# A two-layer decoder trunk on one core: bias put into the mixing's banks, first blocks in turns, token scales by transposes, four early units behind a normed phase

## What is computed

```python
def chunked_gmlp(h, w_in, v_g, w_s, b_s, w_out):
    uv = gelu(h @ w_in); u, v = split(uv, 2)           # 2048 x 4096
    v = rms_norm(v by group of 128 columns, v_g)
    mixed = einsum('gts,bnsgd->bntgd', w_s * causal, v) + b_s.T   # per chunk of 128 tokens
    return (u * mixed) @ w_out                          # 2048 x 2048

for layer in range(2):
    hn = rms_norm(h, pre_mix_g[layer])
    mix = chunked_gmlp(hn, ...) if layer == 0 else attention(hn, K, V) @ b_w_o
    h = h + rms_norm(mix, post_mix_g[layer])
    f = conv_ffn(rms_norm(h, pre_ffn_g[layer]), ...)
    h = h + rms_norm(f, post_ffn_g[layer])
```

## Time and profile before

| | us |
|---|---|
| median of 3 runs (2145.09 to 2146.48) | 2145.13 |
| the profiled execution | 2144.64 |
| its span | 2142.9 |
| TensorE busy | 2132.9 (100%) |
| TensorE weight loads busy | 1829.1 (85%) |
| VectorE busy | 1438.2 (67%) |
| ScalarE busy | 1012.9 (47%) |
| GpSimd busy | 72.0 (3%) |

### The profile page before, as it was taken

How to read it: one execution, slowest core, us unless ns; L and a number is a source line. 1 busy time by engine, 2 the same in 40 slices (tenths; PEclk the granted TensorE clock), 3 DMA queues, 4 the chain that set the end, 5 groups by cost and what they waited for, 6 DMA issues and landing times.

```text
span 2142.9 us, 32178 instructions
## 1 busy us (share of the span) xinstructions
PE 2132.9 (100%) x11289; PEld 1829.1 (85%) x11289; DVE 1438.2 (67%) x1766; ACT 1012.9 (47%) x1167; POOL 72.0 (3%) x97
## 2 busy tenths in 40 slices
PE   9999999999999999999999999999999999999998
PEld 7888888888888888888888888888888888888887
DVE  5676577787877774444765675577877778774444
ACT  5444454444444444443644574464444444444442
POOL 0510010000000000000000000010000000000000
PEclk9999999999999999999999999999999999999999
DMA  8865566666666666555566544656666666666664
GB/s 254 232 188 176 184 179 192 192 188 181 194 192 186 186 207 203 191 191 181 188 190 190 175 153 155 206 170 195 186 177 200 191 189 189 180 220 192 195 195 149
DMA packets 210414, 406.27 MB, mean 190 GB/s; under 512 B 13440, under 2 KB 15904, under 8 KB 209696
## 3 DMA queue, kind: packets, MB, share of 16 engines
q1 hardware_dynamic: 207904, 398.51, 60.9%
q0 software_dynamic: 2384, 6.70, 1.0%
q10 hardware_dynamic: 48, 0.02, 0.0%
HBM read 403.06 MB, written 2.10 MB: 189 GB/s over the span
## 4 chain that ended last, share of the span: by engine, by line
PE 98%; issue 0%; DMA 0%; DVE 0%; ACT 0%; SPq 0%; DVEq 0%; POOLq 0%; POOL 0%; ACTq 0%
PE ps L1433 37%; PE ps L1436 18%; PE ps L1447 13%; PE ps L1449 13%; PE ps L1448 13%; PE ps L1400 1%; PE ps L1403 1%; PE ps L1364 1%; PE ps L1534 1%; PE ps L1367 0%; PE ps L1608 0%; PE ps L1675 0%; PE ps L1646 0%; DMA raw<-in_a_w_in 0%; PE ps L1657 0%
## 5 line engine op out<-in xcount | busy, mean ns | idle before, releaser
L869 DVE TENSOR_TENSOR w_lo<-raw,w_hi 128x1024 fp32r<-128x1024 f32 x744 | 907.6, 1226 | 638.4 <-ACT w_hi L535 632.9
L535 ACT CAST w_hi<-raw 128x1024 fp32r<-128x1024 f32 x750 | 782.2, 1050 | 944.3 <-PE ps L1436 527.6
L1433 PE MATMUL ps<-x_parts,w_hi 128*128 128x512 f32 x3136 | 1089.3, 394 | 0.0
L1436 PE MATMUL ps<-x_parts,w_lo 128*128 128x256 f32 x3136 | 869.7, 277 | 0.0
L1433 PEld LDWEIGHTS ps<-x_parts,w_hi 128*128 128x128 f32 x3136 | 588.1, 188 | 137.1
L1436 PEld LDWEIGHTS ps<-x_parts,w_lo 128*128 128x128 f32 x3136 | 589.1, 188 | 0.0
L1447 PE MATMUL ps<-w_hi,g_parts 128*128 128x512 f32 x704 | 274.0, 389 | 0.0
L1449 PE MATMUL ps<-w_hi,g_parts 128*128 128x512 f32 x704 | 273.9, 389 | 0.0
L1448 PE MATMUL ps<-w_lo,g_parts 128*128 128x512 f32 x704 | 273.9, 389 | 0.0
L1449 PEld LDWEIGHTS ps<-w_hi,g_parts 128*128 128x128 f32 x704 | 132.1, 188 | 27.7
L1448 PEld LDWEIGHTS ps<-w_lo,g_parts 128*128 128x128 f32 x704 | 132.1, 188 | 27.5
(11 more groups left out here) (168 smaller groups left out, 1753.6 us busy)
## 6 DMA issues: line engine op xcount, KB each, us to landing
raw<-in_ffn_w_up SPq DMA_DIRECT2D x352, 512.0 KB, 3.7
raw<-in_ffn_w_down SPq DMA_DIRECT2D x176, 512.0 KB, 4.7
raw<-in_a_w_in SPq DMA_DIRECT2D x62, 512.0 KB, 4.6
raw<-in_a_w_out SPq DMA_DIRECT2D x32, 512.0 KB, 4.7
raw<-in_b_w_q SPq DMA_DIRECT2D x32, 512.0 KB, 4.6
raw<-in_w_k SPq DMA_DIRECT2D x32, 512.0 KB, 4.5
raw<-in_w_v SPq DMA_DIRECT2D x32, 512.0 KB, 4.6
raw<-in_b_w_o SPq DMA_DIRECT2D x32, 512.0 KB, 4.6
```

What stands on the lines that cost most here:

```text
L535: act.copy(w_hi[:, slot, :, :], raw[:, slot, :, :]).then_inc(unit_hi, 1)
L869: dve.tensor_tensor(w_lo[:, slot, :, :], raw[:, slot, :, :], w_hi[:, slot, :, :].bitcast(F32), ALU.subtract).then_inc(unit_split, 1)
L1433: pe.matmul(ps[:, bank + m, :], w_hi[:, slot, kk, m * P:(m + 1) * P], src[:, kt, :, :].rearrange("p a t -> p (a t)"), start=first, stop=False,
L1436: mm = pe.matmul(ps[:, bank + m, 0:T], w_lo[:, slot, kk, m * P:(m + 1) * P], src[:, kt, HI, :], start=False, stop=last, skip_group_check=True)
```

## The change

Four edits, which share names but no place in time but for the token scales.

1. **Bias.** `bias_parts` and its split go. POOL loads the bias, the same for all partitions, into `bias_wide` in four pieces during `gate_u`. ScalarE copies it into the mixing's banks (`place_bias`): four during the last block of `gate_u`, four behind it. TensorE's mixing products add to what lies there. VectorE's addition for the last u block moves in front of the first gates. The next phase waits for two gated groups instead of four.
2. **First blocks in turns.** `load_first_blocks` and `first_blocks` take units of block 0 and block 1 of `gate_v` alternately, so each x tile serves two units; three units, not two, are split half by half; VectorE makes the first cast; the stream's pieces are loaded at greater distances and turned behind units 2, 4, 8 and 12.
3. **Token scales.** `spread` transposes the scales, broadcast along the free dimension; `pre_diagonals` goes. The first one is done before the last unit of the two first blocks.
4. **Behind a normed phase.** `EARLY` = 4 and a twelfth slot; slot 2 is turned before the last tile of the normed phase. VectorE casts the third unit (`third_high`), POOL subtracts unit 1 alone, once `h` is updated in its first quarter, and VectorE unit 2. ScalarE waits for the drained bank before slot 3.

```diff
@@ POOL
+            for q in range(NB):
+                pool.wait_ge(unit_used, gate_u.unit(1) + UK * q)
+                pool.dma_start(bias_wide[:, q * TB:(q + 1) * TB, :],
+                               a_b_spatial[0:1, q * TB:(q + 1) * TB, :].to_broadcast([P, TB, P])
+                               ).then_inc(bias_loaded, 16)
...
-                    if s + 1 < len(NORMED):
-                        unit_low(BEHIND[s], half + 1)
                 if s + 1 < len(NORMED):
+                    pool.wait_ge(h_new[1], NB * s + 1)
+                    unit_low(BEHIND[s], 1)
                     pre_rsqrt(s + 1)
@@ ScalarE
+            def place_bias(g2):
+                if g2 == 0:
+                    act.wait_ge(bias_loaded, 16 * NB)
+                act.copy(ps[:, mixing_bank(g2), :].rearrange("p (g a t) -> p g a t", g=2, a=NH),
+                         bias_wide[:, 2 * g2:2 * g2 + 2, :].unsqueeze(2).to_broadcast([P, 2, NH, P])
+                         ).then_inc(bias_placed, 1)
...
+            act.wait_ge(evacuated, gate_u.block_end)
+            for g2 in range(2):
+                place_bias(G // 4 + g2)
             for g2 in range(2):
                 group_high(g2)
+                place_bias(G // 4 + 2 + g2)
+            gelu_u(LAST)
             units(a_out.first, RING - 1, RING)
-            gelu_u(LAST)
@@ ScalarE, turn_and_split
+                act.wait_ge(evacuated, ph.block0)
+                slot_high(t, (3,))
+                act.wait_ge(unit_hi, ph.first + 3)
                 units(ph.first, 3, RING)
+                slot_high(t, (4, 5))
+                slot_keep(t, (3, 4))
+                slot_high(t, (6, 7))
...
                 units(nxt.first, 0, 2)
-                slot_high(s + 1, (0, 1))
-                slot_keep(s + 1, (0,))
+                slot_high(s + 1, (0, 1, 2))
                 square(s, LAST, (1,))
+                slot_keep(s + 1, (0, 1, 2))
@@ VectorE
+            def third_high(ph):
+                dve.wait_ge(raw_loaded[2], 16 * (ph.first // RING + 1))
+                dve.wait_ge(unit_used, ph.first + 2 - RING + 1)
+                dve.wait_ge(unit_hi, ph.first + 2)
+                dve.tensor_copy(w_hi[:, 2, :, :], raw[:, 2, :, :]).then_inc(unit_hi, 1)
...
             def turn_and_split(t, ph):
-                slot_low(t, (2,))
+                gain_block(t - 1, LAST, (1,))
                 update_first(t - 1)
-                gain_block(t - 1, LAST, (1,))
-                slot_low(t, (3,))
+                slot_low(t, (3, 4))
                 update_stream(t - 1, 1, 1)
-                slot_low(t, (4,))
+                slot_low(t, (5,))
                 update_stream(t - 1, 2, 0)
                 update_stream(t - 1, 2, 1)
-                slot_low(t, (5, 6))
-                dve.wait_ge(unit_split, ph.first + EARLY)
-                units(ph.first, 3, RING)
+                slot_low(t, (6, 7))
+                dve.wait_ge(unit_split, ph.first + 2)
+                units(ph.first, 2, RING)
                 update_stream(t - 1, 3, 0)
                 update_stream(t - 1, 3, 1)
-                slot_low(t, (7,))
+                slot_low(t, (8, 9))
                 units(ph.first, RING, RING + 1)
...
             units(a_out.first, 0, RING - 1)
+            add_low(u_block(LAST), LAST + 1, column_bank(LAST % 2, 1))
             gate_group(0)
             gate_group(1)
-            add_low(u_block(LAST), LAST + 1, column_bank(LAST % 2, 1))
+            scale_tokens(u_block(LAST), gate_u.block0 + LAST, LAST + 1)
             group_low(0)
-            scale_tokens(u_block(LAST), gate_u.block0 + LAST, LAST + 1)
             group_low(1)
@@ TensorE
+                    if u == 1:
+                        turn_slots(t, (3,))
                     if u == EARLY - 1:
-                        turn_slots(t, (3, 4))
+                        turn_slots(t, (4, 5))
...
             def spread(t):
-                pe.wait_ge(diag_ready, t + 1)
+                pe.wait_ge(pre_scaled, t + 1)
                 for half in range(NH):
-                    mm = pe.matmul(ps[:, row_bank(t), half * P:(half + 1) * P], ones_r[:, :].bitcast(F32), diag[:, half, :],
-                                   start=True, stop=True)
+                    mm = pe.transpose(ps[:, row_bank(t), half * P:(half + 1) * P],
+                                      pre_scale[:, half:half + 1].to_broadcast([P, P]), ident[:, :])
...
+            TURNED_BEHIND = {2: range(4, 6), 4: range(6, 10), 8: range(10, 14), 12: range(14, KT)}
+            def first_blocks():
+                for n in range(2 * U):
+                    hb, u = n % 2, n // 2
+                    if n == 2 * U - 1:
+                        spread(0)
+                    if n < OPENING:
+                        opening_unit(n)
+                    else:
+                        pe.wait_ge(unit_split, n + 1)
+                        pe.wait_ge(x_ready, UK * u + UK)
+                        tokens_out_half(gate_v, hb, u, 0, x_parts, n % RING)
+                        tokens_out_half(gate_v, hb, u, 1, x_parts, n % RING).then_inc(unit_used, 1)
+                    turn(0, TURNED_BEHIND.get(n, ()))
...
             for g2 in range(G // 2):
-                bias = bias_parts[:, 2 * g2:2 * g2 + 2, :].unsqueeze(2).to_broadcast([P, 2, NH, P])
-                pe.matmul(ps[:, bank, :].rearrange("p (g a t) -> p g a t", g=2, a=NH), ones_r[:, :], bias,
-                          start=True, stop=False, skip_group_check=True)
+                pe.wait_ge(bias_placed, g2 + 1)
...
-            pe.wait_ge(group_gated, 4)
+            pe.wait_ge(group_gated, 2)
```

More of the change, by code:

```diff
@@ L210, in build_trunk @@
         x_loaded = [sem(f"x_loaded{c}") for c in range(KT // UK)]
-        first_loaded = [sem(f"first_loaded{u}") for u in range(2)]
+        first_loaded = [sem(f"first_loaded{n}") for n in range(3)]
+        first_cast = sem("first_cast")
         first_hi = sem("first_hi")
@@ L395, in load_pair @@
                         k = hb * ph.units + u
[L396 to L401, removed]
+                        sp.wait_ge(unit_split, i * (2 * ph.units) + (ph.first + k - RING + 1))
                         rows = ph.w[u * UK * P:(u + 1) * UK * P, bass.ds(ph.column(i, hb), BLK)]
[L403 to L407, removed]
                         sp.dma_start(raw[:, k % RING, :, :],
@@ L672, in gelu_u @@
                 act.activation(tiles, tiles, ACT.Gelu_apprx_tanh).then_inc(u_ready, 1)
-            U = gate_v.units
-            for b in range(1, NB):
-                units(gate_v.unit(b), NB - 1 if b == 1 else 0, RING)
+            def place_bias(g2):
[4 more added lines that the diff above has]
+                         ).then_inc(bias_placed, 1)
+            U = gate_v.units
+            for b in range(2, NB):
+                units(gate_v.unit(b), 0, 2)
+                if b == 2:
+                    gelu_v(0)
+                units(gate_v.unit(b), 2, RING)
                 gelu_v(b - 1)
@@ L687, in _ @@
                     gelu_u(b - 1)
+                    if b == LAST:
+                        act.wait_ge(evacuated, gate_u.block0 + LAST)
+                        for g2 in range(G // 4):
+                            place_bias(g2)
                     units(gate_u.unit(b), RING + 2, U)
-                if b == 2:
-                    act.wait_ge(bias_loaded, 16)
-                    act.wait_ge(bias_cleared, 1)
-                    act.copy(bias_parts[0:1, :, :], bias_row[:, :, :]).then_inc(bias_hi, 1)
             def group_high(g2):
@@ L1438, in columns_out, with tokens_out_half @@
                         mm.then_inc(unit_used, 1)
-            def tokens_out_half(ph, hb, u, half, src):
-                slot = (hb * ph.units + u) % RING
+            def tokens_out_half(ph, hb, u, half, src, slot=None, tiles=range(UK)):
+                slot = (hb * ph.units + u) % RING if slot is None else slot
                 t0 = half * P
-                for kk in range(UK):
+                for kk in tiles:
                     kt = UK * u + kk
@@ L1463, in last_units @@
                 for u in range(ph.units - RING, ph.units):
-                    tokens_out_half(ph, hb, u, 1, src).then_inc(unit_used, 1)
+                    tokens_out_half(ph, hb, u, 1, src, tiles=range(UK - 1))
+                    if t is not None and u == ph.units - 1:
+                        turn_slots(t, (2,))
+                    tokens_out_half(ph, hb, u, 1, src, tiles=range(UK - 1, UK)).then_inc(unit_used, 1)
                     if t is not None and u == ph.units - 2:
@@ L1560, in products @@
                     for half in range(NH):
-                        mm = pe.matmul(ps[:, half, :], x_parts[:, kt, x_part, half * P:(half + 1) * P],
-                                       w_part[:, u, kk, :], start=(kt == 0 and x_part == HI and w_part is w_hi),
-                                       stop=False)
+                        mm = pe.matmul(ps[:, token_bank(gate_v, hb, half), :],
```

(2 more changed lines are left out.)

189 lines of the change are left out of this document (76 added, 113 removed).

## The result

The changed kernel takes 2163.23 us (median of 6 runs, 2155.18 to 2164.07), the kernel before 2145.24 beside it (6 runs, 2145.09 to 2146.48): a ratio over all runs of 1.0078, 95% interval 1.0068 to 1.0088 (the medians alone give 1.0084). It is slower by 0.8%, where 2141.5 was forecast, with a range of 2138.8 to 2143.8. The profiled execution took 2164.07 around a span of 2162.3.

What follows compares the result with a forecast made beforehand. TensorE was taken as the bound, with 98% of the chain. Mixing -2.3, token scales -0.9, opening -1.4 and behind the normed phases +1.0 made -3.6, from the median 2145.13 to 2141.5 us; range 2138.8 to 2143.8.

Steps and rivals of the forecast that it cites:

- the one that I forecast and priced at 0.4: Behind each normed phase: TensorE waits 0.4 us for the low part of unit 4.
- Mixing: In the mixing, bias copied into the banks removes TensorE's bias products: 6.6 us instead of 9.0, less a 0.1 wait, gain 2.3.
- the round: In the mixing: one of eight equal parts, its eight mixing pieces taking 0.81 us without the bias product.
- The forecast wait of 0.1: In the mixing: ScalarE's fourth late bias copy ends at 194.6, TensorE wants it at 194.5, so it waits 0.1 us.
- late copies: Rival, mixing: at 0.9 us per bias copy the fourth comes at 196.0, 1.5 of 2.3 lost: 2143.0; chance 0.10.
- Token scales: At four spreadings of the scales: two transposes replace four fp32 pieces, 0.22 us less each, 0.9 in all.
- The 0.09 for a spreading: Token scales: by the skill's factor of four the 0.35 us of four pieces becomes 0.09, saving 1.0 over four spreadings.
- Opening: In the first two blocks: earlier first product 0.3, fewer waits 0.9, fewer turnings 0.2; gain 1.4 us, bounds 0.2 to 2.0.
- The burst of spatial loads: After the opening: POOL's `v_gain` and first spatial load leave at about 47, some 10 us later; cost zero, bound 1.5.
- Behind the normed phases: At three places, the new unit order costs 0.25 us each, 0.25 more behind K and V; together +1.0.
- Both forecast waits: Behind each normed phase: TensorE waits 0.2 us at unit 2's second half and 0.4 at unit 4.
- The slower rival: Behind each normed phase VectorE becomes the bound; 2149.9 us if its chain is 2.8 longer per phase; chance 0.05.

Runs made afterwards that it cites:

- only_behind: The kernel before with only the new order behind a normed phase (edit 4 of the change): 2147.13 us, beside 2145.49 for the kernel before.
- only_scales: The kernel before with only the transposed token scales (edit 3 of the change): 2144.64 us, beside 2145.24 for the kernel before.
- behind_and_scales: The kernel before with two edits, the new order behind a normed phase and the transposed token scales: 2167.31 us, beside 2145.24 for the kernel before.
- four_pieces: The changed kernel with its token scales spread as before, by two fp32 products (four pieces in the trace): 2143.49 us, beside 2145.34 for the kernel before.
- wide_first: The changed kernel with both 512-column products of a bank ahead of both 256-column ones in all column phases: 2145.82 us, beside 2145.24 for the kernel before.
- wait_early: The changed kernel with TensorE's wait for unit 4 moved ahead of the last second-half unit, before the eight transposes: 2161.93 us, beside 2145.09 for the kernel before.

## Why the prediction was wrong

**The step that failed** is the last sentence of it: "All of it would be wrong if TensorE's own pieces grew longer, which no row suggests." They grew, by 21 us against terms that sum to 3.6. The sum had put the pace of the column phases, 55% of the chain on the page, at no change. Rows of before did suggest that they can: its `gate_u` stood at 342 instructions in 60 us and its other column phases at 1732 in 300, or 346 in 60, with the same instructions and clock. I counted starts only at the places of the diff and never compared the phases' pace.

Shown: in this order of products the pace has two values; it takes the fourth and the third edit together to lose the quick one (`only_behind`, `only_scales`, `behind_and_scales`, `four_pieces`). Shown by counts, over one trace of each kernel and without `wide_first`: eight transposes with products on both sides were followed by quick pairs in 25 of 25 places, and in the three of `wait_early` wherever the clock was full; four fp32 pieces ended the slow pace in 6 of 6. With a wait between eight transposes and the pairs, 21 of 22 places began slow. The wait is the one that I forecast and priced at 0.4; what it does to the pace had no term. Not settled: what in the chip makes the two cycles, why four transposes differ from four fp32 pieces, and what decides the place in the cycle behind a wait; the runs show a draw.

**The terms.**
- Mixing, forecast -2.3, bounds -1.8 to -2.5: from the last `u` product to the next phase's first it is 9.11 to 9.12 in the seven traces with the old mixing and 7.17 to 7.18 in the eleven with the new, -1.9. The mis-sized number is the round, 0.89 and not 0.81: the pieces start 0.112 apart, eight to a round, and the 0.81 had spanned seven steps between them; that was the lower bound. The copy of 128x512 into PSUM took 0.58, the cast of that size from SBUF to SBUF 0.61 to 0.62. By its sign this agrees with what the Trainium skill ("ScalarE: Activation LUTs", Step-by-step: what each stage is for) says, that ScalarE reaches PSUM faster than SBUF, though copy and cast are not one operation. The forecast wait of 0.1 did not come, but that is the round's doing: the copies ended 5.7 behind the start of the mixing (at 193.8), as forecast (5.8), and the eighth round began 6.2 behind it, not 5.7. Against late copies I had argued that nothing of this size took more than 0.62 on ScalarE; its activations of 128x512 out of PSUM took up to 0.69.
- Token scales, forecast -0.9: two transposes take 0.136 from start to start, the four pieces took 0.363, 4 x 0.227 = -0.9. By itself the edit measured -0.6, within what such a run can tell. The 0.09 for a spreading that the Trainium skill's factor of four gave ("TensorE: Matmul & The Clock Gate", Terms) did not come; 0.14 did, a factor of 2.7.
- Opening, forecast -1.4: the `u` phase starts at 98.6 (median of seven traces with the old opening, 98.3 to 99.9) and 97.4 (eleven, 96.7 to 98.6). With the first spreading's 0.2 taken off, -1.0. In the profiled execution the first product came at 6.20, 0.16 earlier and not 0.3; the second piece of weights landed only at 7.66, before ScalarE's cast of it, and TensorE stood 0.34 for that. The third unit began at 13.07 and the fourth at 16.15, not at 12.0 and 15.2, and the 17th 0.7 earlier than before (54.16 against 54.84), not 1.6. The burst of spatial loads cost nothing: TensorE has no wait there.
- Behind the normed phases, forecast +1.0: `only_behind` measured +1.6. Both forecast waits came in all three places: 0.25 at unit 2 (0.2 forecast) and 0.44 at unit 4 (0.4). What the sum lacked is the slow pace of four units instead of one ahead of the spreading, 3 x 8 x 0.0067 = 0.16 per phase. 1.0 + 3 x (0.05 + 0.04 + 0.16) = 1.75, within 0.2 of the run.

With the sizes measured the sum is -1.9 - 0.9 - 1.0 + 1.6 = -2.2, 2143. `four_pieces` has all edits but the third: -1.3, 2144.0 by the 2145.34 beside it, and it is at 2143.49. The steps held to 0.6 or better each. The slower rival (VectorE as the bound) had the right sign and the wrong cause.

## What to carry to other kernels

Before pricing an edit by the steps around it, compare the pace of the longest phases in the trace with each other: two paces for the same instructions are a risk as large as their difference times the phase. In a kernel bound by one stream of products, an edit far from that stream can move it from one pace to the other; so test each edit also in pairs, and read counts per stretch, not only waits. Here four idle fp32 pieces (0.36 us) near the start of a slow phase of 90 us gave back 1.7, and the kernel is 1.2 faster for them (2139.44 against 2140.67).

## What the hardware showed beyond that

Back-to-back pairs of 512 and 256 columns run at 0.3467 or 0.3534 us at full clock, and keep the one for up to 474 us through loops and block ends. Behind 3.0 us without products TensorE's granted clock was 0.50 in three of three places of `wait_early`, for 3.4 us or more, and behind `a_out` eight transposes at that clock took 1.56 instead of 0.79. In the changed kernel VectorE's cast of 128x1024 from SBUF to SBUF took 0.69, its subtraction of that size with two operands 1.22.
